# Two-layer diffusion trunk: neighbourhood attention by pairs of heads instead of by single heads

## The reference: what is computed

```
# latent queries: 8 x 16 window keys (banded to 8 x 32 = 256 columns, masked) and all 256 context keys
s_loc = einsum('bhcqd,bhicjd->bhcqij', q_blk, k_band) + bias      # masked with -inf outside the window
s_ctx = einsum('bhcqd,bhnd->bhcqn', q_blk, kh_c)
p = softmax(concatenate([s_loc, s_ctx], -1))
out = p_loc . v_band + p_ctx . vh_c
# context queries (first layer only): softmax over the 256 context keys, no bias
```

## Time and profile before

| | us |
|---|---|
| time, median of 3 runs | 4565.77 (4565.65 to 4565.78) |
| the profiled execution's own time | 4563.95 |
| its span | 4562.1 |
| attention, layer 0 (first scores to the next stage's first matmul) | 470.79 to 601.94 |
| attention, layer 1 (the same) | 3044.76 to 3145.20 |
| granted TensorE clock, mean of the span | 0.968 |

### The profile page before, as it was taken

One profiled execution on the slowest core, in us unless ns is written; L12 is line 12 of the kernel. 1 busy time (PEld: TensorE's weight loads), 2 busy tenths in 40 slices (PEclk: granted clock), 3 DMA queues, 4 the chain that ended last, 5 costly groups with the idle time before them and its releaser, 6 DMA issues.

```text
span 4562.1 us, 47007 instructions
## 1 busy us (share of the span) xinstructions
PE 3875.7 (85%) x11600; PEld 1865.6 (41%) x11600; DVE 3238.1 (71%) x8467; ACT 805.5 (18%) x2178; POOL 1542.1 (34%) x1425
## 2 busy tenths in 40 slices
PE   7998898878888888888888869989898888888887
PEld 3435754433333333333333334466543333333332
DVE  3106757888888878878888743075887888888885
ACT  2003321211111111111111121033211111111111
POOL 1100103444444444444444410000344444444442
PEclk8998899999999999999999989979999999999999
DMA  7632127999999999999999961123799999999998
GB/s 273 217 113 63 65 111 319 421 408 398 421 420 394 420 421 393 421 410 388 422 408 409 422 241 56 53 74 125 290 421 413 399 418 421 384 417 420 399 420 339
DMA packets 243595, 1486.16 MB, mean 326 GB/s; under 512 B 24960, under 2 KB 49792, under 8 KB 72688
## 3 DMA queue, kind: packets, MB, share of 16 engines
q0 software_dynamic: 191232, 1385.58, 74.2%
q1 hardware_dynamic: 52208, 98.79, 6.3%
HBM read 1477.87 MB, written 2.21 MB: 324 GB/s over the span
## 4 chain that ended last, share of the span: by engine, by line
PE 40%; DVE 20%; DMA 19%; issue 16%; POOL 2%; DVEq 1%; ACT 1%; SPq 0%; POOLq 0%; ACTq 0%; PEldq 0%
DMA arena<-in_updown,arena 18%; PE ps L820 14%; PE ps L792 6%; PE ps L636 4%; PE ps L651 3%; DVE arena L1527 3%; PE ps L762 3%; DVE arena L1536 2%; POOL arena L1148 2%; PE ps L656 2%; PE ps L729 2%; DVE arena L1496 1%; DVE arena L1501 1%; DVE arena L1499 1%; PE ps L718 1%
## 5 line engine op out<-in xcount | busy, mean ns | idle before, releaser
L820 PE MATMUL ps<-arena 128*128 128x512 f32 x5120 | 2430.4, 613 | 530.0 <-DVE arena L1527 526.9
L1148 POOL DMA_INDIRECT arena<-in_updown,arena x1280 | 1461.4, 1142 | 2051.4 <-PE ps L820 1637.9
L1536 DVE CUSTOM_DVE_ANT_0 arena<-arena 128x1024 bf16<-128x1024 f32 x1280 | 1566.3, 1224 | 363.3 <-DMA arena<-in_updown,arena 317.9
L820 PEld LDWEIGHTS ps<-arena 128*128 128x128 f32 x5120 | 920.7, 191 | 1958.9 <-DVE arena L1527 1132.3
L1055 ACT ACTIVATE arena<-arena 128x1 f32<-128x1 f32 x1280 | 258.9, 203 | 2695.7 <-DVE arena L1536 2695.0
L1527 DVE TENSOR_SCALAR arena<-CN,arena 128x128 f32<-128x128 f32 x1280 | 445.5, 348 | 188.0 <-PE ps L820 158.3
L792 PE MATMUL ps<-arena 128*128 (+1 forms) x1280 | 292.2, 382 | 5.6 <-DVE arena L1433 5.6
L792 PEld LDWEIGHTS ps<-arena 128*128 128x128 f32 x1280 | 244.8, 192 | 72.7 <-issue 43.0
L1142 POOL TENSOR_TENSOR arena<-arena 128x256 f32<-128x256 f32 x64 | 40.7, 668 | 650.3 <-DMA arena<-in_bias 650.3
L636 PE MATMUL ps<-arena 128*128 128x512 f32 (+1 forms) x672 | 239.9, 514 | 2.5 <-DMA arena<-in_w_in 2.5
L636 PEld LDWEIGHTS ps<-arena 128*128 128x128 f32 x672 | 128.1, 194 | 119.0 <-issue 107.3
(11 more groups left out here) (195 smaller groups left out, 2718.7 us busy)
## 6 DMA issues: line engine op xcount, KB each, us to landing
arena<-in_ada_w POOLq DMA_DIRECT2D x40, 1024.0 KB, 5.7
arena<-in_updown,arena POOLq DMA_INDIRECT x1280
arena<-in_wq SPq DMA_DIRECT2D x16, 1024.0 KB, 18.3
arena<-in_w_in SPq DMA_DIRECT2D x6, 2048.0 KB, 10.4
arena<-in_w_in SPq DMA_DIRECT2D x24, 512.0 KB, 4.0
arena<-in_ada_w SPq DMA_DIRECT2D x4, 2048.0 KB, 14.4
arena<-in_bias SPq DMA_DIRECT2D x16, 512.0 KB, 3.9
arena<-in_w_out SPq DMA_DIRECT2D x2, 4096.0 KB, 13.3
```

The costliest lines, as they stand in the source:

```text
L820: mm = e.matmul(ps[hf][:], diag[:, k % 2, :], ring[k % RING][:, D + hf * 512:D + (hf + 1) * 512], start=False, stop=False, skip_group_chec ...
L1148: e.indirect_dma_start(ring[k % RING], None, updown, bass.IndirectOffsetOnAxis(ap=idx16[:, k:k + 1], axis=0)).then_inc(sem(f"rows{k % RING ...
L1536: e.tensor_tensor_reduce(prod[:, k % 2, :], ring[k % RING][:, 0:D], u, 1.0, 0.0, ALU.mult, ALU.add, dots[:, k:k + 1]).then_inc(sem("L.dot_ ...
```

## The change

A unit of work is now a **pair** of heads that lie in the two halves of one 128-row group (heads 2c and 2c+1 of a block). Scores of the pair run as four matmuls, the first head's on array rows 0 to 63, the second's on rows 64 to 127, into two neighbouring PSUM banks. Bias and maxima are each one DVE instruction over both banks. Exponentials, normalisation and transposes stay per job. Values run as eight matmuls with 64 weight columns each, one head into output partitions 0 to 63 and the other into 64 to 127 of the same bank, so that one DVE copy takes both. Score banks become two pairs of banks (0 and 1, 2 and 3), and the mLSTM tiles share banks 4 and 5 with the transposes.

The order of the work changes too. PE at step p: `scores(p)`, `turn(2p-2)`, `turn(2p-1)`, `values(p-2)`. DVE at step p: `add_bias(p)`, `normalise(2p-2)`, `normalise(2p-1)`, `find_max(p)`, `head_norm`, `keep_values(p-3)`. ACT: `keep_probT` twice, then `exponent` twice.

```diff
-SCORE_SLOTS = 3
-OUT_BANK = (3, 6)
-TURN_LAG, VALUES_LAG, KEEP_LAG = 2, 3, 4
+JOB_SLOTS = 4
+OUT_BANK = (6, 7)
...
-                def scores(n):
-                    b, h = att[n]
-                    if n >= SCORE_SLOTS:
-                        e.wait_ge(sem("L.p_exp"), n - SCORE_SLOTS + 1)
-                    bank = ps[n % SCORE_SLOTS]
...
+                def scores(p):
+                    b, c = pairs[p]
+                    if p >= 2:
+                        e.wait_ge(sem("L.p_exp"), 2 * (p - 1))
+                    heads = [(slice(o, o + DH), psum[:, 2 * (p % 2) + o // DH, :]) for o in (0, DH)]
...
+                        for rows, bank in heads:
+                            kb = nk[rows, c, CTX:T].rearrange("p (r w) -> p r w", w=GRID_W)[:, :, BAND_LO[b]:BAND_LO[b] + BAND]
+                            e.matmul(bank[:, 0:LOC], nq[rows, c, at:at + P], kb, start=True, stop=True)
+                    for rows, bank in heads:
+                        mm = e.matmul(bank[:, LOC:512], nq[rows, c, at:at + P], nk[rows, c, 0:CTX], start=True, stop=True)
+                    mm.then_inc(sem("L.s_att"), 1)
...
-                        mm = e.matmul(ps[OUT_BANK[n % 2]][:, 0:P], vband[:, vt, (h // 2) * P:(h // 2 + 1) * P],
-                                      probT[:, n % 2, a * P:(a + 1) * P], start=(a == first), stop=(a == 3))
+                        for o in (0, DH):
+                            mm = e.matmul(ps[OUT_BANK[p % 2]][o:o + DH, 0:P], vband[:, vt, c * P + o:c * P + o + DH],
+                                          probT[:, (2 * p + o // DH) % JOB_SLOTS, a * P:(a + 1) * P], start=(a == first), stop=(a == 3))
...
+                for p in range(len(pairs) + 2):
+                    if p < len(pairs):
+                        scores(p)
+                    if 1 <= p <= len(pairs):
+                        turn(2 * p - 2)
+                        turn(2 * p - 1)
+                    if p >= 2:
+                        values(p - 2)
...
+                def add_bias(p):
+                    b, c = pairs[p]
+                    half, at = 2 * b + c // 2, 2 * (p % 2)
+                    e.wait_ge(sem("L.s_att"), p + 1)
+                    if b < NBAND:
+                        e.wait_ge(sem("L.bias_ready"), half + 1)
+                        local = psum[:, at:at + 2, 0:LOC]
+                        e.tensor_tensor(local, local, biasb[:, half % 2, 2 * (c % 2):2 * (c % 2) + 2, :], ALU.add).then_inc(sem("L.bias_used"), 1)
+
+                def find_max(p):
+                    at, a0 = 2 * (p % 2), 0 if pairs[p][0] < NBAND else LOC
+                    if pairs[p][0] < NBAND:
+                        e.wait_ge(sem("L.bias_used"), p + 1)
+                    e.tensor_reduce(nmax[:, at:at + 2], psum[:, at:at + 2, a0:512], AX.X, ALU.max, negate=True).then_inc(sem("L.nmax_ready"), 1)
+
+                def normalise(n):
+                    s, a0 = n % JOB_SLOTS, 0 if pairs[n // 2][0] < NBAND else LOC
+                    e.wait_ge(sem("L.p_exp"), n + 1)
+                    ch.link(e.reciprocal(rinv[:, s:s + 1], rsum[:, s:s + 1]))
+                    e.tensor_scalar(prob[:, s, a0:512], prob[:, s, a0:512], rinv[:, s:s + 1], None, ALU.mult).then_inc(sem("L.p_ready"), 1)
...
+                for p in range(len(pairs) + 3):
+                    if p < len(pairs):
+                        add_bias(p)
+                    if 1 <= p <= len(pairs):
+                        normalise(2 * p - 2)
+                        normalise(2 * p - 1)
+                    if p < len(pairs):
+                        find_max(p)
+                    k = mlstm_tile_at(p, 1, NT - t0)
                     if k is not None:
                         head_norm(t0 + k)
+                    if p >= 3:
+                        keep_values(p - 3)
```

More of the change, by code:

```diff
@@ L191, with attention_pairs, mlstm_tile_at, turn_items @@
 LATE_KEY_AT = 11
-def attention_jobs(l):
-    return [(b, h) for b in range(NBAND + (NCT if l < L - 1 else 0)) for h in range(NAH)]
-SCORE_SLOTS = 3
-OUT_BANK = (3, 6)
-TURN_LAG, VALUES_LAG, KEEP_LAG = 2, 3, 4
[L205 to L213, removed]
+def attention_pairs(l):
+    return [(b, c) for b in range(NBAND + (NCT if l < L - 1 else 0)) for c in range(NAH // 2)]
+JOB_SLOTS = 4
+OUT_BANK = (6, 7)
+def mlstm_tile_at(p, lag, tiles):
+    k = p - lag
+    return k if 0 <= k < tiles else None
+def turn_items(l):
+    pairs, tiles, items = len(attention_pairs(l)), NT - (0 if l < L - 1 else NCT), []
+    for p in range(pairs + 1):
+        if p >= 1:
+            items += [("job", 2 * (p - 1)), ("job", 2 * (p - 1) + 1)]
+        if mlstm_tile_at(p, 2, tiles) is not None:
+            items.append(("tile", mlstm_tile_at(p, 2, tiles)))
+    return items
 BAND_DMAS = NBAND * (P // BAND)
@@ L417, in build @@
         assert len(ring) == RING
[L419 removed]
+        psum = ctx.enter_context(nc.psum_tensor("psum", [P, 8, 512], F32))
+        ps = [psum[:, i, :] for i in range(8)]
         sems = {}
@@ new lines, in first_key, with keep_probT @@
+                def first_key(n):
+                    return 0 if pairs[n // 2][0] < NBAND else LOC
+                def keep_probT(n):
+                    e.wait_ge(sem("L.pT_mm"), n + 1)
+                    if n >= JOB_SLOTS:
+                        e.wait_ge(sem("L.o_mm"), n // 2 - 1)
+                    bank, a0 = ps[4 + items.index(("job", n)) % 2], first_key(n)
+                    e.activation(probT[:, n % JOB_SLOTS, a0:512], bank[:, a0:512], ACT.Copy).then_inc(sem("L.pT_ready"), 1)
@@ new lines, in exponent @@
+                def exponent(n):
+                    if n % 2 == 0:
+                        e.wait_ge(sem("L.nmax_ready"), n // 2 + 1)
+                    if n >= JOB_SLOTS:
+                        e.wait_ge(sem("L.pT_mm"), n - JOB_SLOTS + 1)
+                    s, a0 = n % JOB_SLOTS, first_key(n)
+                    e.activation(prob[:, s, a0:512], ps[s][:, a0:512], ACT.Exp, bias=nmax[:, s:s + 1],
+                                 accum_out=rsum[:, s:s + 1]).then_inc(sem("L.p_exp"), 1)
+                for p in range(len(pairs) + 1):
+                    if p >= 1:
+                        keep_probT(2 * p - 2)
+                        keep_probT(2 * p - 1)
+                    if p < len(pairs):
+                        exponent(2 * p)
+                        exponent(2 * p + 1)
+                    k = mlstm_tile_at(p, 2, NT - t0)
```

133 lines of the change are left out of this document (44 added, 89 removed).

## The result

The changed kernel takes 4534.75 us (median of 4 runs, 4530.57 to 4536.5) against 4565.71 for the kernel before in the same job; the ratio is 0.9934, with a 95% interval of 0.9921 to 0.9946. That is faster by 31 us; 4584 was forecast, and the range began at 4547. A second set of runs of the same kernel, in another job, gave 4534.51 and 0.9937 [0.9921, 0.9954].

What follows compares the result with a forecast made beforehand. PE was taken to bound steady attention and DVE to set the early pace; steady +23, early -12.6, context +5.5, filling and draining +2 made +18, and 4563.95 + 18 + 1.8 = 4584 us, range 4547 to 4606.

Steps and rivals of the forecast that it cites:

- The clock: Attention: PE's clock falls repeatedly, 60% of the time at 0.50, giving 6.25 us per pair.
- the row at 3008.20: mLSTM heads with small matmuls: PE busy 2.03 of 3.40 us (60%), and the next 6.80 us at clock 0.50.
- The idle 2.14 us: PE idle at 1007.54 among matmuls of 512 columns, where the clock did not fall.
- this ring: Attention's PE and DVE wait on each other through transposes, values, scores, bias and normalisations: 5.02 us per pair at full clock.
- Steady pairs: Attention without mLSTM tiles, about 19.5 pairs in both layers: +1.18 us each, +23.
- Early pairs: Attention while DVE also normalises mLSTM tiles: 7.1 us per pair, 6 x -1.34 and 4 x -1.13, -12.6.
- Context pairs: Eight attention pairs of context queries: 3.6 us each at mixed clock against 2.88, +5.5.
- Filling and draining: Start and end of attention by pairs instead of jobs: +1 us per layer, +2.
- the change of form: Allowance of 0.2 us within the 1.20 us forecast for a pair's values on PE.
- the clock holds: Rival in attention: the clock does not fall, -16 us, so 4550; chance 0.22 with columns overlapping.

Runs made afterwards that it cites:

- more work between the pauses: Changed kernel with scores over all 128 array rows and 0.7 us of unused DVE work between bias and first normalisation in pairs 7 to 15: 4574.25 us.
- whole columns: Changed kernel with each head's values over all 128 columns, one head after the other, and two copies of 64 rows: 4566.15 us, ratio 1.0006.
- whole rows: Changed kernel with each head's scores computed over all 128 array rows instead of its own 64: 4554.3 us, ratio 0.9983.
- Two useless matmuls per pause: Changed kernel with 0.7 us of unused DVE work in pairs 7 to 15, plus two unused 256-column PE matmuls in each pause: 4549.82 us.
- the scores ahead: Changed kernel with PE computing a pair's scores one pair earlier, DVE's order unchanged: 4515.41 us, ratio 0.9897.
- the normalisations first: Changed kernel with both normalisations of the pair before placed ahead of the bias on DVE: 4513.92 us, ratio 0.9894.
- both cuts: Changed kernel with both normalisations ahead of the bias and maxima taken per job with a signal for each: 4512.86 us, ratio 0.9892.

## Why the prediction was wrong

**The step that failed is "The clock"**: "I expect the clock to fall again and again", with 60% of the time at 0.50 and 6.25 us per steady pair. In the changed kernel the clock fell in one ring of each layer, just behind the early part, and in no later one; both steady stretches were at 1.00, and a pair took 4.83. The step took the row at 3008.20 for the nearest, by the share of busy time and the size of the matmuls. The idle 2.14 us at full clock in the same group would have given the right answer here, but was no better guide: 1.98 us in this ring brought the clock down in 17 of 18. I chose between the two with no row that had this ring's pause among this ring's work. The experiments have them (the table above): behind 1.38 to 1.76 us the clock fell in 1 ring of 18, behind 1.71 to 1.87 in 4, behind 1.98 in 17, and behind 1.97 with more work between the pauses in 8. That the changed kernel's pauses were short enough in nearly every steady ring is shown; why single rings fell behind 1.38 and others held behind 1.98 stays open.

The Trainium skill's advice (TensorE: Matmul & The Clock Gate, "Why this matters for your kernels"), no long gaps between bursts, would have given the rival that came nearest. As a rule it is not enough: pauses of 1.98 us, shorter than those that the page warns of, lowered the clock in 17 rings of 18, and the measurement decides.

The other steps, by the sum (+18 forecast; attention measured -24.1):

- *Steady pairs*, forecast +23: 19.5 x (4.83 - 5.07) = -4.7. Of the ring at full clock, 5.02 was forecast and 4.73 measured: values 1.03 instead of 1.20, bias and normalisations 1.80 instead of 2.08 because each starts before the one ahead has ended in the record, transposes 0.2 more.
- *Early pairs*, forecast -12.6 at 7.1: 6 x -1.97 and 4 x -1.81, -19.1. DVE is busy for 34.33 of 38.81 us there; its sum with a tile (6.7) was right to 0.3, the addition for the clock was not needed at 0.89. The clock of this part was 0.79 before; how much of the 19 us it gives was not taken apart.
- *Context pairs*, forecast +5.5: 2.77 against 2.88, -0.9.
- *Filling and draining*, forecast +2: the three above already make -24.7 of the -24.1, so it is about nothing.

Right were: the ring itself, its place and both of its pauses (shown by taking it apart on DVE, -21 us, and on PE, -19); that PE would stand idle some 1.4 us per pair; that the column halves overlap, with 0.17 us too much for the change of form; that scores of a pair cost 1.15. The rival "the clock holds" gave 4550. It missed by 15: 8 in the attention stages (24 instead of 16), the rest outside.

**What was left over.** 6.8 us of the span lie outside attention. I do not ascribe them to the change: over all kernels here, with the same code outside attention, the rest of the span was between 4323.7 and 4336.5 us (before: 4330.5; the changed kernel 4323.7 and 4326.1). What makes it differ was not tried. Whole times of one kernel scatter as widely: the ten executions with whole columns took 4559.65 to 4572.0.

## What to carry to other kernels

When two engines work through one queue each, look in the new order for the ring: an instruction that waits for the other engine and stands ahead of the one that the other engine waits for. Halving the work of an engine that sits in such a ring is worth what stands in the ring and no more (15 us for the row halves, 26 for the column halves); here that only paid for the ring itself, so that steady pairs gained 0.24 us each, and 19 of attention's 24 us came from the early pairs, where DVE set the pace. Putting the line with the late wait last was worth 21 us more. When one ring is cut, add up the next ones before cutting another: an edit that is good alone may close a third.

A pause of PE is to be priced by rows with the same pause in the same kind of work, by several of them, since one ring says little; where none is there, the two levels of the clock are two rivals, not one mixed number.

## What the hardware showed that I had not expected

- Pauses of 1.71 to 1.87 us among the same instructions lowered the clock once in nine rings of layer 0 and three times in nine of layer 1. Pauses of 1.97 us, with whole rows for the scores, lowered it in 8 rings of 18, where 1.98 us with row halves lowered it in 17. And with whole rows it fell once behind a pause of 1.38 us.
- Two useless matmuls per pause made a kernel's attention 24.2 us shorter.
- DVE's TENSOR_SCALAR over 512 values takes 0.49 us alone, and beside POOL's additions up to 0.76 in the changed kernel and up to 1.02 with the scores ahead. That is why steady pairs of 4.72 come with others of 5.0 to 5.2, and in the kernel with the scores ahead with others of 4.97.
- Stages with the same code differed by up to 13 us of the span between kernels. In a comparison of 0.2% this is as large as the effect, and reading the changed stage alone tells more than the whole time: the normalisations first against both cuts, 184.3 against 175.7 us of attention, while the medians differ by 1.
